# A ring of split weights with three places in place of four, in a streaming encoder layer

## The reference

```
proj = rmsnorm(x) @ w_in                      # x_a, x_b, g_a, g_b, 1024 each
c    = conv4(x_a)                             # causal, 4 taps
r, i = sigmoid(c @ w_r + b_r), sigmoid(c @ w_i + b_i)   # 8 heads of 128
a    = exp(8 r log_sigmoid(lam))
h_t  = a_t h_(t-1) + sqrt(1 - a_t^2) i_t c_t  # along the rows
d    = windowed_mean(x_b) - x_b               # windows 2, 4, 8, 16
y_b  = (d @ pool_w) * scale                   # 4 groups of 256
x    = x + (sigmoid(g_a) (h @ w_br_a) + sigmoid(g_b) (y_b @ w_br_b)) @ w_out
x    = x + (silu(rmsnorm(x) @ w_g) * (rmsnorm(x) @ w_u)) @ w_down    # inner width 2816
y    = rmsnorm(x)
```

## Time and profile before

| what | value |
|---|---|
| median of 3 runs | 2878.49 us (2877.73 to 2879.58) |
| profiled execution, its span | 2875.3 us |
| PE matmul busy | 2853.1 us (99%) |
| PE weight load busy | 2821.2 us (98%) |
| DVE busy | 1941.4 us (68%) |
| ACT busy | 1257.3 us (44%) |
| POOL busy | 98.5 us (3%) |
| DMA, mean rate | 123 GB/s |

### The profile page before, as it was taken

How to read it: one execution, slowest core, us unless ns; L and a number is a source line. 1 busy time by engine, 2 the same in 40 slices (tenths; PEclk the granted TensorE clock), 3 DMA queues, 4 the chain that set the end, 5 groups by cost and what they waited for, 6 DMA issues and landing times.

```text
span 2875.3 us, 37697 instructions
## 1 busy us (share of the span) xinstructions
PE 2853.1 (99%) x15028; PEld 2821.2 (98%) x15028; DVE 1941.4 (68%) x2843; ACT 1257.3 (44%) x1762; POOL 98.5 (3%) x188
## 2 busy tenths in 40 slices
PE   8999999999999999999999999999999999999998
PEld 7999999999999999999999999999999999999998
DVE  7867667677666675776666767766666586766565
ACT  6733434258333433573333336634333275343222
POOL 2000000010000000200000001000000010000000
PEclk9999999999999999999999999999999999999999
DMA  7333333333443333243433332433333324333332
GB/s 244 121 125 126 133 117 111 124 110 110 144 137 124 110 121 117 102 137 134 138 117 117 115 118 102 141 128 127 118 124 117 110 100 146 116 110 125 117 118 78
DMA packets 108188, 354.50 MB, mean 123 GB/s; under 512 B 12144, under 2 KB 22768, under 8 KB 108016
## 3 DMA queue, kind: packets, MB, share of 16 engines
q1 hardware_dynamic: 102624, 336.21, 33.7%
q0 software_dynamic: 4096, 13.64, 1.4%
q10 hardware_dynamic: 1296, 2.26, 0.2%
HBM read 339.19 MB, written 12.87 MB: 122 GB/s over the span
## 4 chain that ended last, share of the span: by engine, by line
PE 98%; DMA 1%; DVE 1%; ACT 0%; issue 0%; SPq 0%; DVEq 0%; ACTq 0%
PE ps L405 97%; DMA wraw<-dwm 1%; SPq L279 0%; DVE gb L941 0%; DMA xres<-dx 0%; DVE main L1291 0%; ACT wring L553 0%; PE ps L432 0%; DVE wring L1131 0%; PE ps L433 0%; ACT sring L559 0%; PE ps L450 0%; DVE ylo L946 0%; ACT main L664 0%; DVE sring L1135 0%
## 5 line engine op out<-in xcount | busy, mean ns | idle before, releaser
L405 PE MATMUL ps<-yhi,wring 128*128 128x416 f32 x4800 | 1309.0, 351 | 0.0
L1131 DVE TENSOR_TENSOR wring<-wraw,wring 128x1024 fp32r<-128x1024 f32 x610 | 746.0, 1224 | 302.2 <-ACT wring L553 301.0
L405 PEld LDWEIGHTS ps<-yhi,wring 128*128 128x128 f32 x4800 | 900.7, 188 | 6.8
L405 PE MATMUL ps<-xhi,wring 128*128 128x416 f32 (+1 forms) x3200 | 875.2, 353 | 8.5 <-DVE wring L1131 8.5
L553 ACT ACTIVATE wring<-wraw 128x1024 fp32r<-128x1024 f32 x610 | 641.0, 1051 | 465.5 <-PE ps L405 460.7
L405 PE MATMUL ps<-ylo,wring 128*128 128x416 f32 x2400 | 841.1, 350 | 0.0
L405 PEld LDWEIGHTS ps<-xhi,wring 128*128 128x128 f32 x3200 | 602.2, 188 | 15.0 <-issue 8.5
L405 PE MATMUL ps<-xlo,wring 128*128 128x416 f32 (+1 forms) x1600 | 562.7, 352 | 0.0
L405 PE MATMUL ps<-hhi,wring 128*128 128x416 f32 x1760 | 485.0, 352 | 0.0
L405 PEld LDWEIGHTS ps<-ylo,wring 128*128 128x128 f32 x2400 | 452.2, 188 | 3.7
L405 PEld LDWEIGHTS ps<-hhi,wring 128*128 128x128 f32 x1760 | 329.3, 188 | 2.4
(11 more groups left out here) (171 smaller groups left out, 1603.8 us busy)
## 6 DMA issues: line engine op xcount, KB each, us to landing
wraw<-dwm SPq DMA_DIRECT2D x577, 512.0 KB, 3.2
wraw<-fused SPq DMA_DIRECT2D x40, 512.0 KB, 3.2
xres<-dx POOLq DMA_DIRECT2D x32, 208.0 KB, 3.0
dy<-main POOLq DMA_DIRECT2D x32, 208.0 KB, 2.2
sraw<-dws SPq DMA_DIRECT2D x24, 256.0 KB, 4.3
fused<-main SPq DMA_DIRECT2D x16, 256.0 KB, 4.1
xres<-dx SPq DMA_DIRECT2D x4, 216.0 KB, 5.4
xres<-dx ACTq DMA_DIRECT2D x4, 216.0 KB, 5.8
```

What stands on the lines that cost most here:

```text
L405: mm = nc.tensor.matmul(out, wt[:, c * P:(c + 1) * P], x, start=(first and q == 0), stop=(last and q == 2))
L1131: V.tensor_tensor(wring[:, n % RING, 1, :], wraw[:, n % RAW, :], wring[:, n % RING, 0, :].bitcast(f32), SUB).then_inc(w_lo, 1)
```

## The change

The ring of split weights gets three places (`RING = 3`). `SLOTS` and all places in the engines' orders stay where they are, so at each place ACT and DVE now split the unit that is one number lower: the high part of unit n+3 after unit n, the low part of unit n+2 ahead of the work on unit n. At the start one split of each kind falls away ahead of the loop. SP's numbers follow the ring, all but two: the side units 2 and 3 keep their places ahead of the raw loads 8 and 11.

```diff
-RING = 4
+RING = 3
...
-            at.setdefault(SLOT[("gb", b, last)] + 4 + RAW, []).append(side_unit(b, p) + 4)
+            at.setdefault(SLOT[("gb", b, last)] + RING + RAW, []).append(side_unit(b, p) + 4)
...
-        at.setdefault(SLOT[("w", 0, 2 * g + 1)] + 4 + RAW, []).append(g + 4)
+        at.setdefault(SLOT[("w", 0, 2 * g + 1)] + RING + RAW, []).append(g + 4)
...
-                    if n == SLOT[("w", 0, 2 * g + 1)] + 4 + RAW:
+                    if n == SLOT[("w", 0, 2 * g + 1)] + RING + RAW:
...
                 square("n1", 0, k, xres[:, k, 0:BW[0]])
-                if k == 1:
-                    split_hi(3)
...
             split_lo(1)
-            split_lo(2)
```

## The result

The changed kernel takes 2917.63 us in the median of four runs (2915.15 to 2918.34), against 2878.11 for the kernel before on the same chip (2877.53 to 2879.58). The ratio is 1.0137, with an interval of 1.0123 to 1.0151: 39.5 us slower, where 41.8 were forecast (2920, range 2908 to 2938).

What follows compares the result with a forecast made beforehand. PE, busy 2853.1 of 2875.3 us, was taken to bound the kernel, so new waits add: 9.3 + 19.2 + 5.3 + 2.2 + 5.8 = 41.8 us on 2878.5 gives 2920 us, range 2908 to 2938.

Steps and rivals of the forecast that it cites:

- The rule: Every unit: margin is PE's old start of unit n less old low-part end of unit n+1; negative at 53 units.
- `u(b,1)`: Inner layer, all five blocks: DVE's split after the second norm's reciprocal comes late, 1.06 us each, 5.3 us.
- `g(b,7)`: Inner layer, where DVE sums the next block's squares, not in block 4: 0.55 us each, four times 2.2 us.
- about 40 us: Sign after 84 us: PE waits for DVE's weight split (L1129) this long, in 25 to 35 pieces, none over 3 us.
- The way from DVE to PE: At each new wait: delay from the end of DVE's split to PE's matmul, taken as 0.25 us.
- The gates: Gate stage, blocks 1 to 4: splits within ACT's and DVE's long chain come late, 4.64 x 2 + 5.86 + 4.03 = 19.2 us.
- the first rival: At each place ACT and DVE get late with PE, so waits add: 17.7 us a block, 2959 us; chance 0.08.
- the second rival: Clock falls at new waits, once or twice per gate stage: 5 to 14 us more, 2925 to 2934 us; chance 0.14.
- The cause at `xa`: Start of xa, blocks 1 to 4: DVE's back-to-back instructions, unrelated to the ring, make splits late; 2.33 us each, 9.3 us.
- The opening: Block 0 up to gb(0,2): late low part of xa(0,2) and the load-split loop cost 5.2 to 6.4, taken as 5.8 us.
- I take 0.6 to 1.8: Opening loop: extra lateness in us from side unit 3 coming behind raw load 10 and fuse 2 holding a high part.
- Three places are enough: All units: splits may come sooner than their old places, so PE never waits; 2876 to 2879 us, chance 0.03.

Runs made afterwards that it cites:

- the run with both engines' places: Changed kernel with gate, inner-layer and opening splits moved sooner, ACT's first three squares before its waiting high part, one gate high part behind the roots: 2880.03 us.

## Why the prediction held, step by step

**The rule** (the old start of unit n, less the old end of the next low part) found every place: `xa` 1 and 2, `gb` 0, 1, 2 and 5, `u(b,1)`, `g(b,7)`, and no other from 113 us on but 0.23 us at `b(0,0)`, which was left out. Of the forecast's own signs one was well off: "about 40 us" of waits after 84 us. There are 28.9 of idle time, in 32 pieces of at most 1.85, for the reason given under the profile after. From the first `xa` to the first `a` the distance grew by 6.7, 9.5 and 6.2 us in blocks 1, 2 and 4, for 7.0, 8.2 and 6.4.

**The way from DVE to PE** was mis-sized. I took 0.25 from the earlier trace rows, where PE starts on `w`. There it is still 0.26 (at 51.99 and 62.70 in the changed kernel); at all the new waits for L1129 it is 0.05 to 0.06, and PE's first matmul after the last wait of a group adds 0.11. A regular block, with seven waits in four groups, so costs 8.1 us where 8.6 were forecast. Without the 0.11 and with 0.06: `xa` 2.14 by the working, 2.13 measured (8.5 in four blocks, for 9.3); `u(b,1)` 0.87 and 0.87 (4.4, for 5.3); `g(b,7)` 0.36 and 0.36 (1.5, for 2.2).

**The gates.** Forecast 4.64, 5.86, 4.64 and 4.03; measured 4.42, 7.24, 4.40 and 3.93. That the wait at `gb(b,0)` is a step on the way to that at `gb(b,2)` (`gb(1,2)` is 3.84 us late, in steps of 1.88, 0.11 for the first matmul, 0.12 and 1.74, where the two waits by the working would add to 5.7) is what sets this forecast apart from the first rival, and it held. So did ACT's lateness carried to `gb(b,5)`. The odd one is block 2, where after the wait of 1.78 us at `gb(2,2)` the clock fell:

```profile
1256.05:1259.47 3.42, 1.64 (x9) 1.00 0.00 0
1259.47:1262.88 3.41, 3.41 (x11) 0.50 0.65 211
1262.88:1266.30 3.42, 3.42 (x19) 1.00 0.92 308
```

That is 1.56 us by the start of `gr(2,4)`, beside the 0.11 that the other blocks have there too; without it block 2 is 5.68, and the working with 0.06 gives 5.67. It is the second rival, once and not "once or twice in each gate stage".

**The cause at `xa`** was told by half. "The instructions ahead of them are back to back, and have nothing to do with the ring" is the step that failed, though its number held. DVE's row ahead of them waits 7.28 us for ACT, ACT waits for PE to leave a place, and with four places, or with ACT's squares first, PE doesn't wait at `xa` any more. The number held because the rule takes the old times as fixed to PE's. The high part ahead of the squares waits for the same event of PE in both kernels, the end of `d(b,21)`, and begins 0.26 us after PE's start on `xa(1,0)` in both (606.15 and 611.89). So they were fixed, though not for the reason given.

**The opening** was forecast at 5.8 and measured at 3.84. The rows of the changed kernel, PE first and then ACT:

```profile
21.95 0.47 PE L405 MATMUL ps<-xhi,wring 128*128 128x432 f32 x1 [1.37 <-DVE wring L1129]
...
34.04 0.47 PE L405 MATMUL ps<-xhi,wring 128*128 128x432 f32 x1 [0.92 <-DVE wring L1129]
...
51.99 5.73 PE L405 MATMUL ps<-wring,sring 128*128 128x512 f32 x24 [1.82 <-DVE wring L1126]
```

```profile
44.59 2.19 ACT L553 ACTIVATE wring<-wraw,cst 128x1024 fp32r<-128x1024 f32 x2
46.69 0.62 ACT L559 ACTIVATE sring<-sraw 128x512 fp32r<-128x512 f32 x1
...
85.33 2.14 ACT L676 ACTIVATE tmp<-ps,cst 128x432 f32<-128x432 f32 x4
```

`xa(0,2)` at 21.95 (forecast 21.97) is as told, and fuse 2 is late by 6.6, a little less than the 7 to 8. The term "I take 0.6 to 1.8", for side unit 3 behind raw load 10, is the one that failed: ACT splits it at 46.69 without any wait, and the run that moves it gains nothing. The load on which ACT had waited 1.01 us at 44.15 had now landed, so the late loop took that wait in. The matmul that stood at 84.28 comes at 86.22, 1.9 late and not 2.9 or more. From there the working holds again: with 1.7 of lateness (ACT's sigmoids for 83.62 come at 85.33) and 0.06, 111.13 + 1.7 + 0.06 - 109.03 is 3.86, measured 3.84. That the late loop's saving is all the load's wait is read from the rows and wasn't tried by itself. The clock fall of the earlier trace rows is gone, as was thought possible. And 3.84 is the opening of an execution in which the clock didn't fall there: in three other profiles of the same opening, with one fall or two, `gb(0,2)` is 4.9 (splits at other places), 5.6 (squares first) and 9.1 us (no root) later than before. That the forecast's 5.8 lies among them isn't its merit, since it counted no fall.

**The rivals.** "Each wait is passed on" would have been 17.7 a block; it is 8.1. "Three places are enough" is refuted for this order and holds for another one. With the order of three, a fourth place takes away the waits at `xa` and `g(b,7)` and leaves those at `u(b,1)` and in the gates; so only the latter are a fact about the order alone. That the sum came so near is in part luck, since its errors cancel: the way, 0.19 too long in 18 places (3.4 us), and the opening, 1.8 too long by its lateness, against the first matmul's 0.11, left out in the same 18 places (2.0), and the clock's 1.6. Together they turn 41.8 into 40.2, where the profiled executions have 40.3.

## What to carry to other kernels

When a ring between in-order engines loses a place, take the old trace and set each consumer's start against the old end of the producer's next item: where that is negative lies the price, and within a chain only the last such wait counts. Before a ring is given its place back, look what stands ahead of the producer's late instructions, on both engines that fill it; here a few moved lines were worth 37.6 of 39.5 us. An instruction counts only for what someone waits behind it: the table loads of the root take 1.28 us each, and the 12 were worth 3.9 us, 0.3 each. And before two profiles are compared in a stretch, set their falls of the clock side by side: here they hid a gain of 2.3 us in the opening.

## What the hardware did that I had not expected

PE started 0.05 to 0.06 us after the end of the DVE instruction that it waited for, in all new waits for L1129 (0.26 at the two for L1126, ahead of `fuse`), and its first matmul then took 0.46 us against 0.35.

The granted clock fell to 0.50 after shorter waits than the 2.76 us of the kernel before: after 1.78 us at 1256.84 in the changed kernel, and after 1.81 us in the run with both engines' places:

```profile
46.64:50.05 3.41, 1.60 (x9) 1.00 0.49 187
50.05:53.47 3.42, 3.42 (x10) 0.50 0.94 267
```

But waits of 1.72 and 1.47 us in the same stage of blocks 1, 3 and 4 brought no fall, and the run with four places and the order of three had all the gates' waits and a clock of 1.00 from 13 to 2894 us. Each fall lasted 3.41 us and put PE some 1.6 behind. Which of such waits bring one on was not settled. Where one came early in the gates, in the run with four raw places at 1237.32, all of it went into the waits that followed: `gr(2,2)` came 1.55 later, and `gb(2,1)` and `gb(2,2)` gave back 0.41 and 1.15. The runs with the squares first (at 1233.19) and without the root (at 1241.05) show the same.
